# The state-space mixer's output projection in three rounded products, its low parts stored over the unturned rows

## The chip, the cores and the metric

One core of one Trainium2 chip runs the whole kernel. The metric is device microseconds per execution, lower is better. TensorE is called PE here, VectorE DVE, ScalarE ACT, GpSimd POOL and SyncE SP, as the profile does.

## The reference, cut to what matters

The reference is a network of two blocks on 256 tokens of width 1024, all float32. The second block has two layers; the mixer of its second layer is a bidirectional state-space model (SSD). The change concerns the last line of it, the output projection:

```python
def ssd_mixer(uc, ul, w_in, ..., norm_g, w_out, need_ctx):
    def run(h, s_init, need_y):
        z, xbc, dt = jnp.split(h @ w_in, [SSD_DI, SSD_DI + SSD_CONV_DIM], axis=-1)
        ...
        y = (y_f + y_b[:, ::-1] + xs * d_gr).reshape(b, l, SSD_DI)
        return rms_norm_2(y * jax.nn.silu(z), norm_g) @ w_out, (s_f, s_b)
```

y has 256 rows of 2048 columns, w_out is 2048 x 1024. The rows then go, in "snake" order, through a residual and a layer norm into a squared-ReLU MLP of width 4096.

## The kernel before, in words

The weights of the second block come in chunks of 2 MB. SP loads them into a ring of two slots, W, in the order of plan_chunks; each chunk in two halves of 1024 KB, as soon as the chunk two places ahead of it has been used (L2002 to L2018). For the chunks of the projection, named ("sy", n, c2) (n: half of the output columns, c2: half of the 2048 rows), "used" is the counter part_done for c2 = 0 and the bank ("sy", n, 1) being full for c2 = 1.

Ring (L101) plans the eight PSUM banks: claim waits until the bank's last use has been read, filled until it is full, read until it has been read. plan_block2 (L1581) gives every key its bank.

**The rounds.** The mixer has eight groups of four heads. All engines go through them in step, each in its own written order, and meet at semaphores:

- PE (L2470 to L2481), round g: group_outputs(g) (key "yo", 16 small products, then the two products of 512 columns, "yi", which need the last group's "yi" banks read), group_pre(g+1), group_gate(g+1) (the gate product "sz", 16 float32 products of 256 columns), group_turns(g-1), which turns the finished rows of a group by a product with the permutation, into the bank "yT".
- ACT (L2782 to L2788), round g: segments(g+1) (24 exponentials), state_copy(g+1), gate(g+1) (SiLU of "sz", with a table load), turned_out(g-1), which copies "yT" with the norm's gain into XTOK[:, 2:4].
- DVE (L3288 to L3295), round g: group_weights(g), diagonals(g+1), group_finish(g-1) (the rows of a group: skip, "yo", twice "yi" through YI, gate, squares), state_inputs(g+2).

**The projection.** out_part(n, c2) (L2455) multiplies, for both token tiles t and eight k each, a turned 128x128 tile of XTOK as the stationary operand with 512 columns of the raw chunk in W, all float32. The parts come as (0,0), the last group's turn, (0,1), a small product for the RMS ("rms"), (1,0), (1,1). DVE's residual("sy") (L2838, called at L3312) takes each full bank, scales it by the RMS factor, adds it to x and normalizes each token tile. In its last step sy_between (L3306) makes the first low pieces for the MLP and the low parts of its turned input.

**The MLP's way.** The MLP (ffn, L2163 and L2876) already works with rounded parts: ACT rounds a quarter chunk to float32r into WPH (high_parts, L2530), DVE subtracts it from the raw piece into WPL (low_part, L2871), and PE does three products for each one: high by high, high by low, low by high (L2174, L2191). ACT's order around it is L2789 to L2796: four high pieces, the two roots, split (the turned input with gain, and its rounded part UH), then the other pieces.

ARENA is one region of memory in which the tensors of each phase are carved over those of the last (L1831 to L1850): BDL and CDL first, XTOK (4 x 2048 columns: t = 0 and 1 the finished rows, 2 and 3 the other sequence's rows and later the turned ones), BTOK, SEGW, CBC and so on. The MLP's UH, WPH, UL and WPL lie over the same place.

Of the kernel before, what the change touches and what calls it, by code (L numbers as in the profile page):

```python
# [7 lines left out]
F32 = mybir.dt.float32  # L8
F32R = mybir.dt.float32r
I32 = mybir.dt.int32  # L10
ALU = mybir.AluOpType
# [1569 lines left out]
def plan_block2(full, empty):  # L1581
    r = Ring(full, empty)
    keys = []

    def turned(tag):
        return [("uT", tag, k) for k in range(KT)]

    def split(tag, nt):
        return [("uT", tag, s, j) for s in range(nt // 2) for j in range(4)]

    def plan_ffn(i):

        nt = 4 if i == 0 else 2
        sums = 0
        for kind, b, *rest in mlp_steps():
            if kind == "f1":
                r.plan(("f1", i, 4 * b + rest[0]), rest[0] % (2 if nt == 4 else 4))
            elif rest[1] == 1 and (nt == 4 or b == NB - 1):
                for t in range(nt):
                    r.plan(("f2", i, b, rest[0], t), 2 + sums % 6 if nt == 4 else 4 + sums)  # L1600
                    sums += 1

    keys += split("m0", 4)
    keys += [("ga",)] + [("gl", h, z) for h in range(GH) for z in range(2)]
    keys += [("gq", h) for h in range(GH)] + [("gk", h) for h in range(GH)]

    def along(what, n, ts):
        return [(what, n, t) for t in ts]

    def head_pre(h):  # L1610
        return [("kT", h, z) for z in range(2)] + [("A", h, z) for z in range(2)]

    def head_states(h):
        return [("kvs", h, n) for n in range(3)]

    def head_out(h):
        return [("go", h, s) for s in range(2)]

    for n, k in enumerate(keys):
        r.plan(k, n % 8)  # L1620
    beside = [head_pre(0), head_states(0) + head_pre(1), head_out(0) + head_states(1) + head_out(1),
              head_pre(2) + head_pre(3) + head_states(2) + head_states(3) + head_out(2) + head_out(3)]
    turn = 0
    for (what, half), heads in zip((("gv", 0), ("gv", 1), ("gg", 0), ("gg", 1)), beside):
        for n, k in enumerate(along(what, half, range(4))):
            r.plan(k, 1 + n)
        for k in heads:
            r.plan(k, (5, 6, 7, 0)[turn % 4])
            turn += 1
    keys = []  # L1630
    keys += turned("o0") + [("gy", n, t) for n in range(2) for t in range(4)]
    for n, k in enumerate(keys):
        r.plan(k, (1 + n) % 8)
    for k, b in zip(split("f0", 4), (1, 2, 3, 4, 0, 5, 6, 7)):
        r.plan(k, b)
    plan_ffn(0)
    r.plan(("cw",), 0)
    for (s, j), b in zip(((s, j) for s in range(2) for j in range(4)), (0, 1, 6, 7, 2, 3, 4, 5)):
        r.plan(("uT", "m1", s, j), b)
    keys = [("dt",), ("dtT",)]  # L1640
    conv = []
    for m in range(NX + 2 * SG_ + 1):
        if m == CUM_AT:
            conv += [("cum",), ("cd",)]
        if m < NX + 2 * SG_:
            conv.append(("sc", m))
        if 1 <= m <= NX + SG_:
            conv.append(("xt", m - 1))
    keys += conv
    for n, k in enumerate(keys):  # L1650
        r.plan(k, n % 8)

    def plan_group(g):
        r.plan(("cb", g), g % 2)
        r.plan(("ss", g), 2)
        r.plan(("sz", g), 3)

    plan_group(0)
    for g in range(SG_):
        r.plan(("yo", g), 4 + g % 2)  # L1660
        for t in range(2):
            r.plan(("yi", g, t), 6 + t)
        if g + 1 < SG_:
            plan_group(g + 1)
        if g >= 1:
            r.plan(("yT", g - 1), 2)
    r.plan(("yT", SG_ - 1), 2)
    r.plan(("rms",), 4)
    keys = [("sy", n, t) for n in range(2) for t in range(2)] + split("f1", 2)
    for n, k in enumerate(keys):  # L1670
        r.plan(k, n % 8)
    plan_ffn(1)
    return r
# [64 lines left out]
def block2(nc, io, c, XA, W, WLO, landed, dram_cum, dram_ada):  # L1738

    with ExitStack() as ctx:  # L1740
# [3 lines left out]
        def sem(name):  # L1744
            return ctx.enter_context(nc.semaphore(name))
# [37 lines left out]
        with ExitStack() as conv:  # L1783
            for name, n in (("ahead_of_XHI", 14336), ("XHI", 4096), ("ahead_of_PHI", 5120), ("PHI", 3072)):
                part = conv.enter_context(nc.sbuf_tensor(name, [P, n], F32R))
                if name == "XHI":
                    XHI = part[:].rearrange("p (k n) -> p k n", k=KT)
            PHI = part[:].rearrange("p (b k n) -> p b k n", b=3, k=KT)
        with ExitStack() as gla:
            for name, n in (("ahead_of_XHO", 16384), ("XHO", 4096)):  # L1790
                part = gla.enter_context(nc.sbuf_tensor(name, [P, n], F32R))
            XHO = part[:].rearrange("p (k n) -> p k n", k=KT)
# [118 lines left out]
        w_rdy = sem("b_segment_weights")  # L1911
        y_rdy = sem("b_ssd_out")
        rms_rdy = sem("b_ssd_squares")
        g_hi, g_lo = sem("b_gla_pieces_high"), sem("b_gla_pieces_low")
        g_part = sem("b_gla_partial_piece_used")
        g_xlow = sem("b_gla_x_low_part")
# [175 lines left out]
        def _(pe):  # L2092
# [359 lines left out]
                        last = mm(key, ((2 * q + t) * P, (2 * q + t + 1) * P), XTOK[:, t, k * P:(k + 1) * P], snake[:])  # L2452
                r.fill_done(last, key)

            def out_part(n, c2):  # L2455
                w = weights(("sy", n, c2))
                for t in range(2):
                    key = ("sy", n, t)
                    if c2 == 0:
                        r.claim(pe, key)  # L2460
                    for k in range(KT):
                        kk = c2 * KT + k
                        last = mm(key, (0, CHUNK), XTOK[:, 2 + kk % 2, (kk // 2) * SEQ + t * P:(kk // 2) * SEQ + (t + 1) * P], w[:, k, :],
                                  kk == 0, kk == 15)
                    if c2 == 1:
                        r.fill_done(last, key)
                if c2 == 0:
                    last.then_inc(part_done, 1)

# [5 lines left out]
            for g in range(SG_):  # L2475
# [3 lines left out]
                    group_gate(g + 1)  # L2479
                if g >= 1:  # L2480
                    group_turns(g - 1)  # L2481
            r.read(pe, ("yT", SG_ // 2 - 1))
            out_part(0, 0)
            group_turns(SG_ - 1)
            r.read(pe, ("yT", SG_ - 1))
            out_part(0, 1)
            pe.wait_ge(rms_rdy, 1)
            key = ("rms",)
            r.claim(pe, key)
            r.fill_done(mm(key, (0, 2), snake[:], ST[:, 2:4]), key)  # L2490
            out_part(1, 0)
            out_part(1, 1)
            ffn(1, 2, X_LN[1])

        @block.scalar
        def _(act):
# [270 lines left out]
            def turned_out(g):  # L2767
                key = ("yT", g)
                r.filled(act, key)
                b = bank[r.bank(key)]  # L2770
                for q in range(2):
                    k = 2 * g + q
                    last = nc.scalar.activation(XTOK[:, 2 + q, g * SEQ:(g + 1) * SEQ], b[:, q * SEQ:(q + 1) * SEQ], ACT.Copy,
                                                scale=NGC[:, k:k + 1])
                r.read_done(last, key)

            act.wait_ge(x_whole, 1)
            segments(0)
# [3 lines left out]
            for g in range(SG_):  # L2782
                if g + 1 < SG_:
                    segments(g + 1)
                    state_copy(g + 1)
                    gate(g + 1)
                if g >= 1:
                    turned_out(g - 1)  # L2788
            turned_out(SG_ - 1)  # L2789
            std(SQ_RMS, 0, 2)  # L2790
            high_parts(1, 0, PIECES)
            for t in range(2):
                std(SQ_LN[2] + t, t, t + 1)
            split("f1", 0, 1, 2, UH)
            high_parts(1, PIECES, len(STEPS_F))
            std(SQ_LN[3], 0, 2)  # L2796

        @block.vector
        def _(v):
# [453 lines left out]
            def group_finish(g):  # L3253
# [26 lines left out]
                for t in range(2):  # L3280
                    nc.vector.tensor_tensor_reduce(YI[:, t], xs[:, t], xs[:, t], 1.0 / SDI, 0.0, ALU.mult, ALU.add, RMS[:, t, g:g + 1])

            state_inputs(0)
            r.filled(v, ("sc", NX + 2 * SG_ - 1))
            nc.vector.tensor_tensor(UT[:, :, 0:SEQ], XLO[:, :, 0:SEQ].bitcast(F32), XHI[:, :, 0:SEQ].bitcast(F32), ALU.add).then_inc(x_whole, 1)
# [2 lines left out]
            for g in range(SG_):  # L3288
                group_weights(g)
                if g + 1 < SG_:  # L3290
                    diagonals(g + 1)
                if g >= 1:
                    group_finish(g - 1)
                if g + 2 < SG_:
                    state_inputs(g + 2)  # L3295
            group_finish(SG_ - 1)
            v.drain()
            nc.vector.tensor_reduce(ST[:, 2:4], RMS[:], AX, ALU.add).then_inc(rms_rdy, 1)
            r.filled(v, ("rms",))
            r.read_done(nc.vector.tensor_scalar(ST[:, 0:2], bank[r.bank(("rms",))][:, 0:2], RMS_EPS, None, ALU.add), ("rms",))  # L3300
            v.drain().then_inc(sq_in, 1)
# [2 lines left out]
            v.drain()  # L3304

            def sy_between(n, t):  # L3306
                if n == 1 and t == 1:
                    for q in range(2):
                        low_part(1, q)
                    lows(0, UH, UL, ul_done, 24)  # L3310
# [56 lines left out]
```

## Time and profile before

| | |
|---|---|
| Median of three runs | 2330.67 us (2325.55 to 2337.14) |
| Profiled execution | 2340.91 us, its span 2339.3 us |
| Mean granted clock of PE | 0.948 of full speed |
| PE busy | 2077.0 us (89%), 12086 matmul records |
| DVE busy | 1204.2 us (51%) |
| ACT busy | 727.7 us (31%) |
| POOL busy | 167.0 us (7%) |

The durations below come from the profiled execution, whose time is 10.24 us above the median of the runs. Times of day are microseconds from the start of the span. The state-space rounds lie from about 1947 to 2074, the projection from there to 2131, the last MLP from there to the end. Records of matmuls overlap: the engine is pipelined, and the start-to-start distance is what one costs. One float32 matmul shows as two records.

### The profile page before, as it was taken

Reading aid. Unit: us, or ns where it says so; the run is one execution under the profiler, and the core shown is the slowest. Engines: PE = TensorE matmul, PEld = TensorE weight load, DVE = VectorE, ACT = ScalarE, POOL = GpSimd, SP = SyncE. Lnnn points to the kernel's source line nnn. Section 1 sums busy time; section 2 is a strip of 40 time slices with the busy share of each in tenths; the row PEclk is TensorE's granted clock in tenths of the full one; section 3 lists DMA queues with packets and bytes.
Section 4 is the critical chain, followed back from the end, with each engine's and each line's share of the span. In section 5 each row is a group of like instructions: output and inputs, shape, how many; then the busy total and the mean of one; then the engine's idle time right before and its main releaser. Section 6 shows DMA issues by size and latency. Waiting matters only on the chain.

```text
span 2339.3 us, 32520 instructions
## 1 busy us (share of the span) xinstructions
PE 2077.0 (89%) x12086; PEld 1470.9 (63%) x12086; DVE 1204.2 (51%) x2131; ACT 727.7 (31%) x1317; POOL 167.0 (7%) x155
## 2 busy tenths in 40 slices
PE   6999888888998748886999899999989988998997
PEld 4787432325786412333788778888877776765996
DVE  3464411115463401114738587666666886745766
ACT  3453200103452200003433331221135545722332
POOL 2001100001001100002441300000000000000000
PEclk9989999999999969998999899999999998999999
DMA  7459699984469669984221223222222234324552
GB/s 226 154 209 330 236 404 389 391 312 134 170 235 338 247 262 359 400 320 154 71 77 67 77 90 126 108 85 96 80 99 73 92 128 142 126 73 160 191 191 107
DMA packets 151940, 440.42 MB, mean 188 GB/s; under 512 B 10368, under 2 KB 12848, under 8 KB 143456
## 3 DMA queue, kind: packets, MB, share of 16 engines
q1 hardware_dynamic: 143424, 415.87, 47.9%
q0 software_dynamic: 8352, 22.39, 3.3%
q8 instruction: 101, 1.65, 0.3%
q14 instruction: 63, 0.52, 0.1%
HBM read 534.52 MB, written 1.21 MB: 229 GB/s over the span
## 4 chain that ended last, share of the span: by engine, by line
PE 40%; DVE 6%; ACT 4%; DVEq 2%; issue 1%; DMA 1%; ACTq 0%; POOL 0%; SPq 0%; POOLq 0%
PE bank L2101 24%; PE bank L2192 11%; PE bank L2243 4%; DVE ARENA L3211 1%; ACT ARENA L2753 1%; PE bank L2106 1%; DVEq L2827 0%; ACT UT L2524 0%; ACTq L2527 0%; DVE XA L2828 0%; DMA W<-in_ffn_w 0%; ACT ARENA L2746 0%; DVEq L3213 0%; ACT ARENA L2501 0%; DVE XA L2826 0%
## 5 line engine op out<-in xcount | busy, mean ns | idle before, releaser
L2537 ACT ACTIVATE WPH<-W 128x1024 fp32r<-128x1024 f32 x128 | 135.5, 1063 | 399.5 <-PE bank L2101 199.9
L2101 PE MATMUL bank<-UH,WPH 128*128 128x512 f32 (+1 forms) x512 | 174.5, 341 | 5.6 <-DVE WPL L2873 2.4
L2101 PE MATMUL bank<-UL,WPH 128*128 128x512 f32 (+1 forms) x512 | 173.2, 338 | 0.0
L2101 PE MATMUL bank<-UH,WPL 128*128 128x512 f32 (+1 forms) x512 | 173.0, 338 | 0.0
L2873 DVE TENSOR_TENSOR WPL<-W,WPH 128x1024 fp32r<-128x1024 f32 x128 | 153.6, 1219 | 17.8 <-ACT WPH L2537 17.8
L1426 DVE TENSOR_TENSOR H<-SG,bank 128x256 f32<-128x256 f32 x24 | 10.1, 421 | 289.7 <-ACT SG L1013 289.7
L2192 PE MATMUL bank<-WPH,MHH 128*128 128x512 f32 x384 | 149.5, 389 | 0.0
L2192 PE MATMUL bank<-WPL,MHH 128*128 128x512 f32 x384 | 149.5, 389 | 0.0
L2192 PE MATMUL bank<-WPH,MHL 128*128 128x512 f32 x384 | 149.4, 389 | 0.0
L675 PE MATMUL bank<-W,XG 128*32 128x512 f32 x768 | 98.6, 660 | 50.3 <-DMA W<-in_expert_w_up 38.8
L2101 PE MATMUL bank<-ARENA 128*128 128x64 f32 (+4 forms) x528 | 108.9, 367 | 19.2 <-DVEq L3251 7.6
L675 PE MATMUL bank<-WA,XG 128*32 128x512 f32 x768 | 95.6, 642 | 24.7 <-DMA WA<-in_expert_w_up 24.7
L2101 PEld LDWEIGHTS bank<-UH,WPH 128*128 128x128 f32 x512 | 98.2, 192 | 19.4 <-issue 3.7
L2101 PEld LDWEIGHTS bank<-ARENA 128*128 128x128 f32 (+1 forms) x528 | 83.4, 211 | 39.6 <-issue 19.5
L712 PE MATMUL bank<-WC,H 128*32 128x512 f32 x768 | 89.0, 604 | 21.1 <-DMA WC<-in_expert_w_down 15.4
L1013 ACT ACTIVATE SG<-bank 128x256 f32<-128x256 f32 x24 | 9.2, 383 | 314.9 <-PE bank L675 314.9
L2101 PEld LDWEIGHTS bank<-UL,WPH 128*128 128x128 f32 x512 | 98.3, 192 | 10.1
L2101 PEld LDWEIGHTS bank<-UH,WPL 128*128 128x128 f32 x512 | 98.3, 192 | 10.0
L2101 PE MATMUL bank<-XHI,PHI 128*128 128x512 f32 (+2 forms) x264 | 99.9, 378 | 3.5 <-DVE XLO L2835 2.4
L508 PE MATMUL bank<-W,XT 128*128 128x512 f32 x192 | 89.9, 629 | 11.5 <-DMA W<-in_w_in 7.1
L2101 PE MATMUL bank<-XHI,WLO 128*128 128x512 f32 (+2 forms) x264 | 97.5, 369 | 0.0
L675 PEld LDWEIGHTS bank<-W,XG 128*32 128x32 f32 x768 | 25.2, 119 | 114.5 <-issue 66.7
(445 smaller groups left out, 4341.1 us busy)
## 6 DMA issues: line engine op xcount, KB each, us to landing
WC<-in_expert_w_down SPq DMA_DIRECT2D x32, 2048.0 KB
W<-in_ffn_w SPq DMA_DIRECT2D x64, 1024.0 KB, 6.6
W<-in_ada_w SPq DMA_DIRECT2D x48, 1024.0 KB, 7.3
WA<-in_expert_w_gate SPq DMA_DIRECT2D x16, 2048.0 KB
WA<-in_expert_w_up SPq DMA_DIRECT2D x16, 2048.0 KB
W<-in_expert_w_gate SPq DMA_DIRECT2D x16, 2048.0 KB
W<-in_expert_w_up SPq DMA_DIRECT2D x16, 2048.0 KB
WC<-in_expert_w_down SPq DMA_DIRECT2D x32, 1024.0 KB
```

Source lines behind the costliest of these rows:

```text
L508: last = nc.tensor.matmul(bank[r.bank(key)][:, 0:n], lhs[k], rhs[k], start=(k == 0), stop=(k == len(lhs) - 1))
L675: last = nc.tensor.matmul(bank[r.bank(key)][32 * g:32 * g + 32, :], xg[:, 4 * part + k, col:col + 32], WA[part][:, g, :, k, :], start=(par ...
L712: last = nc.tensor.matmul(bank[r.bank(key)][32 * g:32 * g + 32, :], H[i // MQ][:, f, 32 * g:32 * g + 32], WC[:, g, f, n * CHUNK:(n + 1) * ...
L1426: r.read_done(nc.vector.tensor_tensor(H[q // MQ][:], SG[q // MQ][:].rearrange("p (n f) -> p f n", f=2), bank[r.bank(key)][:, EH:2 * EH].re ...
L2101: return nc.tensor.matmul(bank[r.bank(key)][0:rows, cols[0]:cols[1]], lhs, rhs, start=start, stop=stop)
L2106: return nc.tensor.transpose(bank[r.bank(key)][0:m, j * P:j * P + k], src, ident[0:k, 0:k])
L2192: last = nc.tensor.matmul(bank[r.bank(key)][:, :], a, x[:, k, :], start=first and k == 0 and z == 0, stop=last_block and kp == 1 and k == ...
L2243: last = nc.tensor.matmul(bank[r.bank(key)][:, :], x[:, kk, tok], a[:, k, :], start=kp == 0 and k == 0 and z == 0, stop=kp == 3 and k == 1 ...
L2537: nc.scalar.activation(piece_view(WPH, q), piece_src(i, q), ACT.Copy).then_inc(hi_done, 1)
L2753: last = nc.scalar.activation(SEGD[:, jt, z, h, :], SEGD[:, jt, z, h, :], ACT.Exp, bias=NCUM[:, jt, col:col + 1])
L2873: nc.vector.tensor_tensor(piece_view(WPL, q), piece_src(i, q), piece_view(WPH, q).bitcast(F32), ALU.subtract).then_inc(lo_done, 1)
L3211: last = nc.vector.scalar_tensor_tensor(acc, src, CW[:, m, k:k + 1], acc, ALU.mult, ALU.add)
```

## The change

Both operands of the projection are taken apart into a rounded (float32r) high part and the low rest, and each product becomes three. The parts and their places:

- YH is the turned rows' high part, in the place of XTOK[:, 2:4], written by ACT in turned_out. YL is the low part, in the place of XTOK[:, 0:2], the finished but unturned rows, of which a group is free once it is turned. DVE writes it in a new turned_low(g), out of the same bank, after turned_out(g).
- SYH0, SYH1 and SYH2 take the high part of a chunk of weights, written by ACT in four pieces (out_weights_high); the low part goes to the slot of WLO, by DVE (out_weights_low).
- The bank "yT" is now read by DVE after ACT, and moves from bank 2 to g % 2 (3 for group 6).
- In the rounds, turned_low(g-2) stands on DVE between diagonals(g+1) and group_finish(g-1).
- out_part takes pairs of k and waits for each pair's low parts; (1,1) is done first for token tile 0, then for tile 1.
- On ACT two high pieces of the MLP instead of four come ahead of the split, and they wait for the end of the projection.

```diff
@@ plan_block2
-            r.plan(("yT", g - 1), 2)
+            r.plan(("yT", g - 1), g % 2 if g < SG_ - 1 else 3)
@@ block2
+        with ExitStack() as mixed:
+            SYH2 = mixed.enter_context(nc.sbuf_tensor("SYH2", [P, KT, CHUNK], F32R))
+            YL, YH = [mixed.enter_context(nc.sbuf_tensor(name, [P, 2, SG_ * SEQ], F32R)) for name in ("YL", "YH")]
+            SYH = [mixed.enter_context(nc.sbuf_tensor(f"SYH{q}", [P, KT, CHUNK], F32R)) for q in range(2)] + [SYH2]
@@ PE
-            def out_part(n, c2):
-                w = weights(("sy", n, c2))
-                for t in range(2):
-                    key = ("sy", n, t)
-                    if c2 == 0:
-                        r.claim(pe, key)
-                    for k in range(KT):
-                        kk = c2 * KT + k
-                        last = mm(key, (0, CHUNK), XTOK[:, 2 + kk % 2, (kk // 2) * SEQ + t * P:(kk // 2) * SEQ + (t + 1) * P], w[:, k, :],
-                                  kk == 0, kk == 15)
-                    if c2 == 1:
-                        r.fill_done(last, key)
+            def out_part(n, c2, ts=range(2), kps=range(4)):
+                ci = SY.index((n, c2))
+                lo = WLO[:, number[("sy", n, c2)] % SLOTS]
+                for kp in kps:
+                    pe.wait_ge(sy_lo, 4 * ci + kp + 1)
+                    pe.wait_ge(yl_rdy, 4 * c2 + kp + 1)
+                    for t in ts:
+                        key = ("sy", n, t)
+                        if c2 == 0 and kp == 0:
+                            r.claim(pe, key)
+                        for k in (2 * kp, 2 * kp + 1):
+                            kk = c2 * KT + k
+                            c0 = (kk // 2) * SEQ + t * P
+                            for z, (y, w) in enumerate(((YH, SYH[ci % 3]), (YH, lo), (YL, SYH[ci % 3]))):
+                                last = nc.tensor.matmul(bank[r.bank(key)][:, :], y[:, kk % 2, c0:c0 + P], w[:, k, :],
+                                                        start=kk == 0 and z == 0, stop=kk == 15 and z == 2, skip_group_check=True)
+                        if c2 == 1 and kp == 3:
+                            r.fill_done(last, key)
                 if c2 == 0:
                     last.then_inc(part_done, 1)
...
-            r.read(pe, ("yT", SG_ // 2 - 1))
             out_part(0, 0)
             group_turns(SG_ - 1)
-            r.read(pe, ("yT", SG_ - 1))
             out_part(0, 1)
...
             out_part(1, 0)
-            out_part(1, 1)
+            out_part(1, 1, (0,))
+            out_part(1, 1, (1,))
@@ ACT
-                    last = nc.scalar.activation(XTOK[:, 2 + q, g * SEQ:(g + 1) * SEQ], b[:, q * SEQ:(q + 1) * SEQ], ACT.Copy,
+                    last = nc.scalar.activation(YH[:, q, g * SEQ:(g + 1) * SEQ], b[:, q * SEQ:(q + 1) * SEQ], ACT.Copy,
                                                 scale=NGC[:, k:k + 1])
-                r.read_done(last, key)
+                last.then_inc(yh_rdy, 1)
+
+            def out_weights_high(ci):
+                n = number[("sy", *SY[ci])]
+                act.wait_ge(landed[n % SLOTS], 32 * (n // SLOTS + 1))
+                if ci == 1:
+                    r.filled(act, ("yo", SG_ - 1))
+                if ci == 2:
+                    r.filled(act, ("yi", SG_ - 1, 1))
+                if ci == 3:
+                    act.wait_ge(part_done, 1)
+                for kp in range(4):
+                    if ci == 0 and kp == 2:
+                        r.filled(act, ("yo", SG_ - 2))
+                    nc.scalar.activation(SYH[ci % 3][:, 2 * kp:2 * kp + 2, :], W[:, n % SLOTS, 2 * kp:2 * kp + 2, :], ACT.Copy).then_inc(sy_hi, 1)
...
+                if g == SG_ - 1:
+                    out_weights_high(0)
                 if g >= 1:
                     turned_out(g - 1)
+            out_weights_high(1)
             turned_out(SG_ - 1)
+            out_weights_high(2)
             std(SQ_RMS, 0, 2)
-            high_parts(1, 0, PIECES)
-            for t in range(2):
-                std(SQ_LN[2] + t, t, t + 1)
+            out_weights_high(3)
+            std(SQ_LN[2], 0, 1)
+            r.filled(act, ("sy", 1, 1))
+            high_parts(1, 0, 2)
+            std(SQ_LN[2] + 1, 1, 2)
             split("f1", 0, 1, 2, UH)
-            high_parts(1, PIECES, len(STEPS_F))
+            high_parts(1, 2, len(STEPS_F))
@@ DVE
+            def turned_low(g):
+                key = ("yT", g)
+                v.wait_ge(yh_rdy, g + 1)
+                for q in range(2):
+                    k = 2 * g + q
+                    last = nc.vector.scalar_tensor_tensor(YL[:, q, g * SEQ:(g + 1) * SEQ], bank[r.bank(key)][:, q * SEQ:(q + 1) * SEQ],
+                                                          NGC[:, k:k + 1], YH[:, q, g * SEQ:(g + 1) * SEQ].bitcast(F32), ALU.mult, ALU.subtract)
+                r.read_done(last, key)
+                v.drain().then_inc(yl_rdy, 1)
+
+            def out_weights_low(ci):
+                n = number[("sy", *SY[ci])]
+                for kp in range(4):
+                    v.wait_ge(sy_hi, 4 * ci + kp + 1)
+                    nc.vector.tensor_tensor(WLO[:, n % SLOTS, 2 * kp:2 * kp + 2, :], W[:, n % SLOTS, 2 * kp:2 * kp + 2, :],
+                                            SYH[ci % 3][:, 2 * kp:2 * kp + 2, :].bitcast(F32), ALU.subtract).then_inc(sy_lo, 1)
...
                 if g + 1 < SG_:
                     diagonals(g + 1)
+                if g >= 2:
+                    turned_low(g - 2)
                 if g >= 1:
                     group_finish(g - 1)
...
+            out_weights_low(0)
             group_finish(SG_ - 1)
+            turned_low(SG_ - 2)
             v.drain()
             nc.vector.tensor_reduce(ST[:, 2:4], RMS[:], AX, ALU.add).then_inc(rms_rdy, 1)
+            out_weights_low(1)
+            turned_low(SG_ - 1)
+            out_weights_low(2)
...
             def sy_between(n, t):
+                if n == 0 and t == 1:
+                    out_weights_low(3)
```

## Rows read from the trace of the kernel before

**Rows 1.** The page: the span, and busy time and share by engine.

```profile
span 2339.3 us, 32520 instructions
PE 2077.0 (89%) x12086; PEld 1470.9 (63%) x12086; DVE 1204.2 (51%) x2131; ACT 727.7 (31%) x1317; POOL 167.0 (7%) x155
```

**Rows 2.** Busy time by stretch: three rounds, the projection, two stretches around stalls.

```profile
core 0: us, PE busy (x) PEld busy (x) DVE busy (x) ACT busy (x) POOL busy (x), PEclk, DMA share, GB/s
1985.67:2001.51 15.84, 15.84 (x85) 12.90 (x84) 12.21 (x26) 11.49 (x30) 1.05 (x2) 1.00 0.18 57
2001.51:2018.36 16.85, 15.86 (x85) 12.90 (x84) 14.22 (x29) 11.49 (x30) 1.05 (x2) 1.00 0.58 196
...
2051.05:2066.89 15.84, 15.84 (x85) 12.90 (x84) 10.86 (x22) 11.49 (x30) 0.00 (x0) 1.00 0.00 1
...
2089.00:2131.00 42.00, 41.31 (x98) 18.38 (x98) 7.97 (x15) 6.11 (x9) 0.00 (x0) 1.00 0.42 150
...
1760.00:1770.00 10.00, 6.83 (x33) 5.31 (x32) 6.14 (x11) 6.80 (x9) 0.00 (x0) 1.00 0.00 0
2162.20:2165.60 3.40, 3.32 (x16) 3.32 (x17) 2.99 (x7) 0.00 (x0) 0.00 (x0) 0.51 0.46 164
```

**Rows 3.** PE in order of time: start, us; in brackets the idle time before.

```profile
2007.08 2.82 PE L2101 MATMUL bank<-ARENA 128*128 128x512 f32 x8 [0.99 <-DVE YI L3268]
...
2073.97 13.90 PE L2101 MATMUL bank<-W,ARENA 128*128 128x512 f32 x32
...
1764.13 0.66 PE L2106 MATMUL bank<-ident,ARENA 128*128 128x128 f32 x4 [3.17 <-ACT ARENA L2716]
...
2162.28 0.58 PE L2101 MATMUL bank<-UH,WPH 128*128 128x256 f32 x1 [2.39 <-DVE WPL L2873]
```

**Rows 4.** The chain that ended last: start, us, what.

```profile
2039.77 49.00 PE bank L2101 x220
...
2089.68 41.70 PE bank L2101 x98
...
2162.28 7.42 PE bank L2101 x48
2169.71 10.91 PE bank L2192 x48
2180.61 11.51 PE bank L2101 x96
```

**Rows 5.** Groups of instructions by form, PE, from 2073.9 to 2131.5.

```profile
L2101 PE MATMUL bank<-W,ARENA 128*128 128x512 f32 x128 | 55.6, 594 | 0.9 <-ACT ARENA L2773 0.9
```

**Rows 6.** ACT in order of time.

```profile
2018.61 1.28 ACT L2501 ACT_TABLE_LOAD   x1 [5.32 <-PE bank L2101]
...
2020.39 0.83 ACT L2773 ACTIVATE ARENA<-bank,NGC 128x256 f32<-128x256 f32 x2
...
2125.68 3.90 ACT L2537 ACTIVATE WPH<-W 128x1024 fp32r<-128x1024 f32 x4 [21.40 <-DMA W<-in_ffn_w]
```

**Rows 7.** DVE in order of time.

```profile
2003.47 0.76 DVE L3260 TENSOR_TENSOR ARENA<-ARENA,DROW 128x256 f32<-128x256 f32 x2
...
2004.92 0.75 DVE L3268 TENSOR_TENSOR YI<-bank,EC 128x256 f32<-128x256 f32 x2
...
2066.23 0.76 DVE L3260 TENSOR_TENSOR ARENA<-ARENA,DROW 128x256 f32<-128x256 f32 x2
...
2072.42 0.76 DVE L3260 TENSOR_TENSOR ARENA<-ARENA,DROW 128x256 f32<-128x256 f32 x2
...
2131.41 0.75 DVE L2850 SCALAR_TENSOR_TENSOR ARENA<-bank,ST,MB 128x512 f32<-128x512 f32 x1 [0.66 <-PE bank L2101]
...
2144.00 1.22 DVE L2873 TENSOR_TENSOR WPL<-W,WPH 128x1024 fp32r<-128x1024 f32 x1
...
2173.08 4.62 DVE L2873 TENSOR_TENSOR WPL<-W,WPH 128x1024 fp32r<-128x1024 f32 x4
```

**Rows 8.** SP's DMA issues in order of time.

```profile
2117.67 14.65 SPq L2018 DMA_DIRECT2D W<-in_ffn_w  x4
```

More of the change, by code:

```diff
@@ L1913, in block2 @@
         rms_rdy = sem("b_ssd_squares")
+        yh_rdy, yl_rdy = sem("b_ssd_turned_high"), sem("b_ssd_turned_low")
+        sy_hi, sy_lo = sem("b_ssd_out_weights_high"), sem("b_ssd_out_weights_low")
+        SY = [(n, c2) for n in range(2) for c2 in range(2)]
         g_hi, g_lo = sem("b_gla_pieces_high"), sem("b_gla_pieces_low")
```

## The prediction, made before the change was run

> **What bounds the kernel now.** The page comes first: TensorE (PE) is busy for 89% of the span, so a saving on PE may count, but only where PE is the last to finish [rows 1]. The stage table then splits the eight rounds over the state-space groups. From the end of one gate product to the end of the next a round lasts 15.84 or 16.85 us, 15.84 to 15.86 of it PE, at a granted clock of 1.00 [rows 2]. So PE bounds the rounds, but barely: the 1.0 us missing in every other round is a wait on VectorE (DVE) in the PE timeline, just before the products called "yi" [rows 3]. The DVE step named there is a product written to YI out of a bank (L3268), and in the chain of waits PE alone goes on from that point through the output projection, except for the 0.9 us from 2088.77 to 2089.68, in which ScalarE (ACT) copies the last turned group [rows 4]. After the projection the chain goes by DVE and ACT into the MLP.
>
> **The projection itself: a gain.** The four parts of out_part are 64 float32 matmuls of 512 columns, which the trace shows as 128 records, 55.6 us in all, 13.85 a part from start to start [rows 5]. The change makes 192 rounded ones of them, in the pattern that L2192 has already (high by high, high by low, low by high): 48 of those take 10.91 us at full clock [rows 4]. So each part falls from 13.85 to 10.91 us; over four parts this saves 11.8 us. The loads of weights are hidden in both rows' pace. The trace thus says 0.79 of the old time. The Trainium skill ("FP8 and Floating Point Precision", TensorE Precision Notes) counts true FP32 as four passes; three of four would give 0.75, a saving of 13.9 us instead of 11.8, and the sum below would be 2.1 us better. The trace has a row for each form, so 0.79 stands.
>
> **Splitting the weights.** ACT rounds each chunk in 4 pieces, 3.90 us by the same copies ahead of the MLP [rows 6]; DVE subtracts in 4 pieces, 4.62 us [rows 7]. That is 15.6 us of ACT and 18.5 of DVE more. Between 2089 and 2131 they are busy for only 7.97 (DVE) and 6.11 us (ACT) [rows 2], and PE needs a quarter of a chunk only every 2.73 us (10.91 / 4), where DVE makes one in 1.15 (4.62 / 4). That hides behind PE except at the first piece of a part, below. Each chunk still follows its slot's release: SP issues at 2117.67, and ACT, waiting for the landing, starts at 2125.68, 8.0 us later [rows 6, 8].
>
> **The low rows, in the round: a loss.** Each round g from 2 to 7 now has turned_low(g-2) on DVE ahead of group_finish(g-1). It waits for turned_out(g-2), which ACT does only after gate(g). Behind that wait stands the finish, and for the finish's reads of YI waits PE's "yi" of round g. I follow one round, counted from the end of gate(g) on PE (the turn at 2018.36):
> - ACT: table load from 2018.61, gate copy, turned copies to 2021.22, so 2.86 us after that end [rows 2, 6].
> - DVE: turned_low, two scalar_tensor_tensors of 256 columns out of a bank. No row has that form from a bank; the pair at L3268 takes 0.75 us, and twice the one of 512 columns at L2850 would be 1.50 [rows 7]. I take 0.85, nearest to the pair, and 0.13 for drain and hand-over: the finish starts at 3.84.
> - From the finish's start to PE's "yi": 2003.47 to 2007.08, 3.61 us [rows 3, 7].
> - PE from "yi" to the end of the next gate: 2007.08 to 2018.36, 11.28 us [rows 2, 3].
>
> Together 18.73 us, a circle PE, ACT, DVE, PE in which nothing overlaps. Before, DVE began the finish at 2003.47, 1.96 us after the gate's end [rows 2, 7], without asking ACT. No slack covers this: PE already waits, or just doesn't, at "yi". So each of the six rounds has a PE stall of 18.73 - 15.85 = 2.9 us. What else ACT and DVE do in a round (they are busy for 11.49 and at most 14.22 us of it [rows 2]) then ends before PE asks for it, and leaves the chain.
>
> Place by place: gate(2) ends at 1985.67 as before. Five rounds of 18.73 put the end of gate(7) at 2079.32 (before 2066.89 [rows 2]), and with the sixth stall "yi" of group 7 starts at 2086.8. turned_low(5) and finish(6) then end at 2089.35, since a finish takes 6.19 us (2066.23 to 2072.42) [rows 7]; DVE's first low piece (1.2) lets PE begin the projection at 2090.55, against 2073.97 before [rows 3]. **This costs 16.6 us.**
>
> **From there on.** Part (0,0) ends at 2101.5 and the last turn at 2102.4. DVE has meanwhile done low(0), finish(7), turned_low(6), the sum, and the first piece of low(1) at 2102.6; part (0,1) goes from there to 2113.6. The old 0.9 us wait for ACT is gone: the last group's low rows (2107) are needed only at 2110.8. Chunk (1,0) lands at 2101.5 + 8 = 2109.6, its first low piece is there at 2111.9, PE asks at 2113.7. Chunk (1,1) lands at 2121.6; its first low piece waits rather for the two residuals of n = 0 (three steps like L2850's 0.75 us each [rows 7]) and comes at 2123.9, PE asks at 2124.6. Both fit, by 1.8 and 0.7 us. Part (1,1) by token halves ends at 2135.5, against 2131.4 [rows 4, 7]: **4.1 us later.** This is 16.6 lost, 11.8 gained by the matmuls, some 0.7 by the smaller waits. The bank changes cost nothing: every new claim comes after a read that precedes YI's on DVE.
>
> **Into the MLP.** Only two high pieces are rounded before the split now; the third follows it on ACT and takes 1.0 us (3.90 / 4), so DVE's low piece starts 0.4 us later than in the old order, where it began at 2144.00 right behind the last low part of x [rows 7], and this is on the chain. +0.4. Sum: **+4.5 us** at an undisturbed clock. Its bounds: turned_low from 0.75 to 1.5 us, six times, is -0.6 to +3.9, so +3.9 to +8.4.
>
> **The clock.** Six stalls of 2.9 us are new. A stall of 2.39 us was followed by a stretch at 0.51, the lower level, 1.2 GHz, and 48 matmuls took 7.42 us there against 5.76 (half of 11.51), a loss of 1.7; a stall of 3.17 us after denser work left the clock at 1.00 [rows 2 to 4]. I let two of the six stalls end so: +3.4. The Trainium skill ("TensorE: Matmul & The Clock Gate", HAM oscillation) says that only longer idle gaps than these throttle it; by that rule nothing is added and the time would be 2335.2. The trace has a counterexample at 2.39 us, so the measurement decides.
>
> Forecast: 4.5 + 3.4 = +7.9 us. The rows are of one execution with 2340.91 us (span 2339.3 [rows 1]); the median of the runs is 2330.67, and the difference is set upon that: **2338.5 us**.
>
> **Rivals.**
> 1. The clock stays up in all six stalls: +4.5, 2335.2 us. For it: the 3.17 us stall [rows 3]. Chance 0.17.
> 2. Slower beyond doubt: the stalls throttle in nearly every round. Six times 1.7 on the circle is +10.0, with 4.5 together +14.5, 2345.2 us; from the fifth on it exceeds 0.5%. For it: the shorter stall of 2.39 us did it [rows 3]; against it, each is followed by 15.8 us of dense work. The dear turned_low belongs here too. Chance 0.27.
> 3. Faster: the wait on ACT doesn't reach PE, because finish(g-1) finds its reads done early enough. Then the sum is -11.8 - 0.7 + 0.4 = -12.1, 2318.6 us. For it: PE's share, 89%. Against it: PE waited there even before [rows 3]. Chance 0.07.
> 4. Forecast as above, one to four throttled stalls: 0.49.
>
> That the change doesn't do what it says, I see no way for: the number of matmuls follows from the loops.
>
> **How the numbers follow.** A measurement of this kernel tells about 0.5%, 11.7 us, from nothing. Faster by more: rival 3, 0.07, less a little because it lies so near the bound: 0.06. Slower by more: rival 2's 0.27 and the upper edge of the forecast, 0.05: 0.32. The rest, 0.62, is the same. Range: from 2324 (below rival 1, since three runs spread over 2325 to 2337) to 2350 (rival 2 with a dear turned_low in part); rival 3 and the far end of rival 2 are left out.
>
> **What would show it.** Rounds 3 to 7, end of gate to end of gate: 18.7 us each (right) or 16 (rival 3). PE idle ahead of "yi" about 2.9 us, DVE idle ahead of turned_low, for ACT, 3 to 4 us once the rounds have settled. The four parts: 192 matmuls, 43.6 us. PE's first sy matmul at about 2090.6, its last at 2135.5. Clock below 1.00 in some rounds. I am wrong if the rounds keep 16 us, or if PE waits for low pieces or landings inside parts (1,0) and (1,1).

## The result, and the profile after

| | before | changed |
|---|---|---|
| Median of ten runs each | 2330.02 us | 2342.97 us |
| Ratio, 95% interval | | 1.0063 [1.0046, 1.008] |
| Span of the profiled execution | 2339.3 us | 2346.0 us |
| PE busy | 2077.0 us | 2065.6 us |
| DVE busy | 1204.2 us | 1229.0 us |
| ACT busy | 727.7 us | 743.6 us |

The change makes the kernel slower by 0.63%, 14.7 us of 2330, although PE is busy for 11.4 us less. (The ratio isn't the quotient of the two medians, which are 12.95 us or 0.56% apart; that lies within its interval.) The rounds show why. First the busy time by stretch, from the end of one gate product to the end of the next, from gate(2) to gate(7) (they answer to [rows 2]), then the stretch up to shortly before the first matmul of the projection:

```profile
core 0: us, PE busy (x) PEld busy (x) DVE busy (x) ACT busy (x) POOL busy (x), PEclk, DMA share, GB/s
1976.63:1997.97 21.34, 18.39 (x85) 14.13 (x84) 14.83 (x30) 11.61 (x30) 1.05 (x2) 0.84 0.14 50
1997.97:2018.46 20.49, 17.54 (x85) 13.78 (x84) 14.00 (x28) 11.61 (x30) 1.05 (x2) 0.92 0.45 154
2018.46:2038.96 20.50, 17.55 (x85) 13.76 (x84) 14.00 (x28) 11.61 (x30) 1.05 (x2) 0.92 0.16 52
2038.96:2059.46 20.50, 17.55 (x86) 13.75 (x85) 14.00 (x28) 11.61 (x30) 0.00 (x0) 0.92 0.30 103
2059.46:2079.95 20.49, 17.54 (x85) 13.73 (x84) 10.25 (x20) 11.61 (x30) 0.00 (x0) 0.92 0.00 0
2079.95:2091.20 11.25, 8.30 (x50) 6.54 (x49) 7.65 (x17) 6.39 (x8) 0.00 (x0) 0.87 0.53 188
```

A round takes 20.5 us (the first 21.3) where it took 15.8 or 16.9. Two things are new in it. PE is idle for 2.95 us (20.50 less 17.55), and its busy time has itself grown from 15.86 to 17.55 us, because the mean clock of the round is 0.92 instead of 1.00. Both stand in the PE timeline of one round:

```profile
2018.46 1.05 PE L2108 MATMUL bank<-snake_perm,ARENA 128*128 128x128 f32 x8
2019.36 3.68 PE L2108 MATMUL bank<-ARENA 128*128 128x64 f32 x32
2025.99 4.51 PE L2108 MATMUL bank<-ARENA 128*128 128x512 f32 x8 [2.95 <-DVE YI L3301]
2030.34 1.88 PE L2108 MATMUL bank<-MB,ARENA 128*128 128x512 f32 x4
2032.06 7.07 PE L2108 MATMUL bank<-W,UT 128*128 128x256 f32 x32
```

The eight records of "yi" and "cb" behind the stall take 4.51 us; they took 2.82 [rows 3]. The 1.7 us more are the lower clock, right after the idle time. Behind the first stall, the stretch shows it without a mixture: 0.50, the lower level, 1.2 GHz.

```profile
1984.15:1987.50 3.35, 3.35 (x4) 1.48 (x5) 3.03 (x10) 3.35 (x12) 0.00 (x0) 0.50 0.00 0
```

The other stalls of the six are as long (2.95 us) and were all followed by the lower level: 5.36 us for these eight records behind the first, 4.51 behind the next four, and 2.98 for the last group's four (1.98 at full clock in the run filler3, below). The chain of waits shows the circle, one turn of it:

```profile
2018.71 0.87 ACT L2514
2019.58 0.42 issue
2020.00 0.60 ACT ARENA L2514
2020.60 0.74 ACT YH L2786 x2
2021.36 0.48 DVE YL L3321
...
2022.38 0.43 DVE ARENA L3293
...
2025.99 13.15 PE bank L2108 x44
```

PE ends the gate, ACT loads its table, copies the gate and then the turned rows (YH); only then DVE makes the low rows (YL) and starts the finish. From "yi" on PE has 13.15 us of work to the end of the next gate. DVE has been waiting for ACT all the while, as its timeline shows:

```profile
2013.28 2.50 DVE L3269 TENSOR_TENSOR ARENA<-ARENA,NEGM 128x512 f32<-128x512 f32 x4
2021.36 0.88 DVE L3321 SCALAR_TENSOR_TENSOR YL<-bank,NGC,YH 128x256 fp32r<-128x256 f32 x2 [5.59 <-ACT YH L2786]
2022.38 0.76 DVE L3293 TENSOR_TENSOR ARENA<-ARENA,DROW 128x256 f32<-128x256 f32 x2
```

The projection did get its gain. The groups by form, from 2088 to 2139 (against [rows 5]), and the chain from the first part on:

```profile
L2477 PE MATMUL bank<-SYH,YH 128*128 128x512 f32 x64 | 25.5, 398 | 0.2 <-DVE WLO L3330 0.2
L2477 PE MATMUL bank<-WLO,YH 128*128 128x512 f32 x64 | 25.4, 396 | 0.0
L2477 PE MATMUL bank<-SYH,YL 128*128 128x512 f32 x64 | 25.2, 394 | 0.0
```

```profile
2091.99 11.09 PE bank L2477 x48
2103.08 0.89 PE bank L2108 x8
2103.97 11.12 PE bank L2477 x48
2115.11 0.37 SPq L2025
2115.52 8.63 DMA W<-in_ssd_w_out
2124.18 1.07 ACT SYH L2802
2125.27 1.24 DVE WLO L3330
2126.55 11.48 PE bank L2477 x48
2138.05 0.75 DVE ARENA L2883
```

A part takes 11.1 us instead of 13.9. The busy times of the three groups overlap and can't be added. For one part, the last, the chain goes by its chunk's landing; the wait it leaves on PE is short, 0.16 us idle in the timeline.

Where the time went, from the places above and those of before [rows 2 to 4, 7]:
- From the end of gate(2) to that of gate(7): 81.22 us (1985.67 to 2066.89) became 103.32 (1976.63 to 2079.95), +22.1.
- From there to the first projection matmul: 7.08 (to 2073.97) became 11.80 (to 2091.75), +4.7.
- The projection until DVE takes the last bank: 57.44 (to 2131.41) became 46.30 (to 2138.05), -11.1.
- From there to the end of the span: 207.9 both times.

That is +15.7 us. The rest of the difference of the spans, -9.0, lies ahead of gate(2), in code that the change doesn't touch. How much that code varies from one execution to the next can be read off the nine kept traces: gate(2) ends anywhere between 1966.97 and 1985.67. The stretch from there to the last bank's read (145.74 us before, 161.42 changed) leaves that out, and is used below beside the ratios, as what one execution of each kernel shows.

### The profile page after: what moved, and what is told of

It reads as the page before. It is cut to its first block, busy times and chain, and to the rows that moved or that the text cites. A ratio compares the mean times of both kernels' runs of the same rounds, so it can differ in the third digit from the quotient of the medians.

```text
span 2346.0 us, 32725 instructions
## 1 busy us (share of the span) xinstructions
PE 2065.6 (88%) x12150; PEld 1486.1 (63%) x12150; DVE 1229.0 (52%) x2163; ACT 743.6 (32%) x1333; POOL 166.9 (7%) x155
## 4 chain that ended last, share of the span: by engine, by line
PE 40%; DVE 6%; ACT 3%; DVEq 2%; issue 1%; DMA 1%; ACTq 0%; SPq 0%; POOL 0%; POOLq 0%
PE bank L2108 23%; PE bank L2199 11%; PE bank L2250 4%; PE bank L2477 1%; DVE ARENA L3244 1%; PE bank L2113 1%; ACT ARENA L2514 0%; DVEq L2860 0%; DMA W<-in_ssd_w_out 0%; ACT UT L2537 0%; ACTq L2540 0%; DVE XA L2861 0%; DMA W<-in_ffn_w 0%; DVEq L3246 0%; DVE XA L2859 0%
## 5 line engine op out<-in xcount | busy, mean ns | idle before, releaser
L2108 PE MATMUL bank<-ARENA 128*128 128x64 f32 (+4 forms) x528 | 119.5, 390 | 34.7 <-DVE YI L3301 17.7
L675 PE MATMUL bank<-WA,XG 128*32 128x512 f32 x768 | 88.9, 604 | 24.8 <-DMA WA<-in_expert_w_up 24.8
L2108 PE MATMUL bank<-XLO,PHI 128*128 128x512 f32 (+2 forms) x264 | 97.2, 368 | 0.0
```

The source lines that it names most:

```text
L675: last = nc.tensor.matmul(bank[r.bank(key)][32 * g:32 * g + 32, :], xg[:, 4 * part + k, col:col + 32], WA[part][:, g, :, k, :], start=(par ...
L2108: return nc.tensor.matmul(bank[r.bank(key)][0:rows, cols[0]:cols[1]], lhs, rhs, start=start, stop=stop)
```

## The experiments

The seven variants were timed against the kernel before on the same chip. The medians of before there were 2328.25 us (low_rows_inside to before_wait) and 2327.62 us (low_rows_behind to before_time); the row of the changed kernel is that of the result, with 2330.02 us before. So the ratios are what to compare between rows, and not the medians. The last column is the stretch in each profiled execution from the end of gate(2) to DVE's start on the last bank of the projection. The theories: **A**, the wait for ACT's copy closes a circle through PE, ACT and DVE, and its stalls also lower the clock. **B**, what costs is DVE's 1.0 us for the low rows, wherever it stands. **C**, the whole added work is too much for ACT and DVE.

| kernel | ratio to before, 95% | median us | gate(2) to last bank, us |
|---|---|---|---|
| before | | | 145.74 |
| changed | 1.0063 [1.0046, 1.008] | 2342.97 | 161.42 |
| low_rows_inside | 0.9954 [0.9936, 0.9971] | 2316.37 | 134.70 |
| no_low_rows | 0.9963 [0.9945, 0.998] | 2315.64 | 134.73 |
| filler3 | 1.0028 [1.0013, 1.0043] | 2331.99 | 150.97 |
| before_wait | 1.0084 [1.0066, 1.0103] | 2344.47 | 163.20 |
| low_rows_behind | 0.9958 [0.9936, 0.998] | 2320.16 | 140.34 |
| filler1 | 1.0043 [1.0022, 1.0064] | 2337.42 | 158.00 |
| before_time | 1.0028 [1.0008, 1.0048] | 2334.42 | 154.90 |

### low_rows_inside: the same work, behind the read that PE waits for

```diff
-                if g >= 2:
-                    turned_low(g - 2)
                 if g >= 1:
-                    group_finish(g - 1)
+                    group_finish(g - 1, g - 2 if g >= 2 else None)
@@ group_finish(g, low=None)
                         if z == 1:
                             r.read_done(last, key)
+                    if z == 1 and low is not None:
+                        turned_low(low)
                     v.drain()
                     nc.vector.tensor_tensor(xs, xs, YI[:], ALU.add)
```

> turned_low(g-2) moves on DVE from ahead of group_finish(g-1) to within it, behind the second read of the yi banks; all else as in the changed kernel. Theory A (the circle PE, ACT, DVE, PE that the wait for the turned copy closes costs 2.95 us a round, and each stall lowers the clock for another 1.7): rounds go back to 15.8 and 16.9 us at a granted clock of 1.00, the first sy matmul comes about 123 us after the first yo matmul instead of 149, and the whole takes about 26 us less than the changed kernel, about 2318, ratio to before 0.995. Theory B (the price is the DVE time of the low rows, 1.0 us a round, wherever it stands): the rounds stay longer than 16.9 us, ratio near 1.005. Theory C (DVE and ACT get too much work in all): PE waits for weight pieces or exponents in the rounds, ratio about 1.00.

Measured: ratio 0.9954 [0.9936, 0.9971], where the changed kernel has 1.0063: 25 us faster than that, 11 us faster than the kernel before. Of the versions that make the whole output it has the lowest ratio. Three of its rounds:

```profile
1976.41:1992.27 15.86, 15.86 (x85) 12.90 (x84) 13.03 (x28) 11.48 (x30) 1.05 (x2) 1.00 0.18 60
1992.27:2009.11 16.84, 15.86 (x86) 12.90 (x85) 14.98 (x31) 11.49 (x30) 1.05 (x2) 1.00 0.59 194
2009.11:2024.96 15.85, 15.85 (x85) 12.90 (x84) 13.01 (x28) 11.49 (x30) 1.05 (x2) 1.00 0.18 56
```

These are the rounds of before to 0.02 us, with the low rows made in them (DVE is busy for 13.0 and 15.0 us instead of 12.2 and 14.2). B falls: the same DVE work costs nothing in the rounds once the read that PE waits for comes first. C falls as well.

### no_low_rows: the ceiling

```diff
-                if g >= 2:
-                    turned_low(g - 2)
...
-            turned_low(SG_ - 2)
...
-            turned_low(SG_ - 1)
...
-                last.then_inc(yh_rdy, 1)
+                r.read_done(last, key)
...
-                    pe.wait_ge(yl_rdy, 4 * c2 + kp + 1)
+                    r.read(pe, ("yT", 4 * c2 + kp))
...
-                            for z, (y, w) in enumerate(((YH, SYH[ci % 3]), (YH, lo), (YL, SYH[ci % 3]))):
+                            for z, (y, w) in enumerate(((YH, SYH[ci % 3]), (YH, lo), (YH, SYH[ci % 3]))):
```

> The changed kernel without turned_low: the low rows are not made, the third product reads the high rows instead, so the low rows' share is left out of the output; the number of matmuls and the weights' parts are as in the changed kernel. Theory A: rounds of 15.8 and 16.9 us, clock 1.00, the four parts 46 us, about 2318 us, ratio 0.995. Theory B: the same here, so this run gives the ceiling that the other one is held against; if the ratio is above 1.00, the loss is in the projection or the weights, not in the rounds.

This kernel leaves the low rows out: its third product reads the high rows again, and its output lacks their share. Measured: 0.9963 [0.9945, 0.998]. This and low_rows_inside can't be told apart by their ratios, and the stretch from gate(2) to the last bank is 134.73 us here and 134.70 there. So low_rows_inside has all there is to get by making the low rows free, and the loss of the changed kernel against it (161.42 us in that stretch) lies in where the low rows stand.

### filler3 and filler1: work instead of idleness

```diff
                 r.read(pe, ("ss", g))
+                for _ in range(3 if g >= 2 else 0):
+                    nc.tensor.matmul(bank[2][:, :], CDL[:, g, 0:P], SSB, start=True, stop=True)
```

filler1 has 1 in place of 3.

> The changed kernel with three more float32 matmuls of 512 columns a round, on rounds 2 to 7, between the yo products and the yi products, into the bank of the states, which is free there: 2.6 us of PE work inside a stall of 2.95 us. Theory A with the clock lowered by idleness: stall 0.35 us or so, clock 1.00 in rounds 3 to 7, a round 18.8 us instead of 20.5, some 10 us less than the changed kernel, ratio to before about 1.002. Rival: the lower clock has another cause than the idle PE; then the rounds stay at 20.5 us or grow, ratio 1.006 or more.

> As filler3 with one filler matmul a round instead of three: 0.87 us of work in the stall, 2.1 us of it left idle. before_wait had stalls of 1.94 us, of which about half were followed by the lower clock. If the idle length decides: rounds of 18.8 us and of 20.5 us mixed, 2 to 4 of the six lowered, 3 to 7 us less than the changed kernel, ratio about 1.004. If any work in the stall is enough: as filler3, ratio 1.0028. If none: as the changed kernel, 1.006.

filler3 measured 1.0028 [1.0013, 1.0043], 8 us below the changed kernel by the ratios and 10.5 by the stretch from gate(2) to the last bank, with 18 float32 matmuls more. Two of its rounds and its stall:

```profile
1985.71:2004.44 18.73, 18.50 (x91) 13.88 (x90) 13.99 (x28) 11.61 (x30) 1.05 (x2) 1.00 0.49 168
2004.44:2023.18 18.74, 18.51 (x91) 13.88 (x90) 14.00 (x28) 11.61 (x30) 1.05 (x2) 1.00 0.17 57
```

```profile
2011.88 2.85 PE L2108 MATMUL bank<-ARENA 128*128 128x512 f32 x8 [0.23 <-DVE YI L3303]
```

The round is 18.74 us, the circle without its clock price, and the clock is at 1.00 in all five rounds. So the lower clock came of PE's idleness, and cost 1.76 us a round (2.60 in the first). filler1 measured 1.0043 [1.0022, 1.0064]. In its profiled execution 1.94 us were left idle:

```profile
1982.32:2001.06 18.74, 16.80 (x88) 13.12 (x86) 14.82 (x30) 11.61 (x30) 1.05 (x2) 1.00 0.17 57
2001.06:2021.49 20.43, 18.48 (x87) 13.74 (x86) 13.99 (x28) 11.61 (x30) 1.05 (x2) 0.92 0.45 154
```

Of the five rounds shown by the stretches, the first was at 1.00 and the four others at 0.92. The sixth group's four records took 3.57 us against 1.98 in filler3, so that five of six stalls were followed by the lower clock, where I had expected two to four. This execution was the slowest of the twelve (2334 to 2350 us), and the spread of some 15 us leaves room for others with fewer; the ratio lies where it was expected, but its interval overlaps those of filler3 and of the changed kernel, so only the trace tells them apart.

### before_wait and before_time: the wait and the work, each alone, in the kernel before

```diff
+                if g >= 2:
+                    r.read(v, ("yT", g - 2))
                 if g >= 1:
                     group_finish(g - 1)
```

> The kernel before, with nothing added but a wait: in rounds 2 to 7 DVE waits, ahead of group_finish(g-1), until ACT has copied the turned rows of group g-2. No low rows, no rounded products. Theory A: rounds of 17.8 us at full clock (2.95 + 3.61 + 11.28), a PE stall of 2.0 us ahead of yi, projection 10 us later than before, and up to 20 us later if each stall lowers the clock; ratio 1.004 to 1.009. Theory B (it is the DVE time of the low rows, not the wait): rounds as before, ratio 1.000.

```diff
+                if g >= 2:
+                    for q in range(2):
+                        xs = XTOK[:, q, (g - 1) * 256:g * 256]
+                        nc.vector.scalar_tensor_tensor(YI[:, q], xs, NGC[:, q:q + 1], xs, ALU.mult, ALU.subtract)
+                    v.drain()
                 if g >= 1:
                     group_finish(g - 1)
```

> The kernel before, with two idle scalar_tensor_tensors of 256 columns and a drain (1.0 us of DVE) in the place of turned_low, in rounds 2 to 7, and no wait: DVE time alone. Theory A: the chain ACT, DVE, PE of two rounds grows by 1.0 us, PE stalls of 1 to 2 us in every other round, 3 us in all, ratio 1.001, against 1.0084 for the wait alone. Theory B, that DVE's time is what costs: ratio 1.004 or more.

before_wait, one wait and no work, costs as much as the whole change does on balance, with the gain in the projection counted: 1.0084 [1.0066, 1.0103] against 1.0063 [1.0046, 1.008]. Four of the five stretches from gate(2) to gate(7), the fourth left out:

```profile
1971.32:1992.07 20.75, 18.81 (x86) 14.29 (x85) 14.06 (x28) 11.61 (x30) 1.05 (x2) 0.84 0.13 52
1992.07:2012.68 20.61, 18.67 (x85) 14.29 (x84) 13.22 (x26) 11.61 (x30) 1.05 (x2) 0.83 0.44 153
2012.68:2030.48 17.80, 15.86 (x86) 12.91 (x85) 13.22 (x26) 11.50 (x30) 1.05 (x2) 1.00 0.17 60
...
2048.27:2067.76 19.49, 17.55 (x86) 13.65 (x85) 9.38 (x18) 11.61 (x30) 0.00 (x0) 0.91 0.00 0
```

17.80 us at full clock is the circle without the low rows, as worked out. The low rows' own DVE time adds the rest, 0.94 us a round, to the 18.74 of filler3. The stalls of these five rounds are 1.94 us long; three of the rounds were slowed, by 1.69 to 2.95 us of PE time (the fourth was like the third, at 1.00, and the sixth stall, 1.92 us, was followed by 1.00 too).

before_time's two idle operations take 0.88 us, as turned_low's do, though they don't read a bank. It measured 1.0028 [1.0008, 1.0048], where I had written 1.001. Its stretches:

```profile
1967.11:1985.62 18.51, 17.55 (x85) 13.49 (x84) 15.64 (x32) 11.62 (x30) 1.05 (x2) 0.91 0.18 58
1985.62:2001.29 15.67, 15.67 (x85) 12.83 (x84) 11.37 (x24) 11.49 (x30) 1.05 (x2) 1.00 0.55 190
2001.29:2022.14 20.85, 18.73 (x85) 14.28 (x84) 18.99 (x39) 11.61 (x30) 1.05 (x2) 0.84 0.17 60
```

```profile
1972.65 4.51 PE L2101 MATMUL bank<-ARENA 128*128 128x512 f32 x8 [0.96 <-DVE YI L3268]
2007.99 5.46 PE L2101 MATMUL bank<-ARENA 128*128 128x512 f32 x8 [2.12 <-DVE YI L3268]
```

The stalls are in every other round and as long as expected (0.96, then 2.12 us). What I had left out is again the clock: each was followed by the lower level. The ratio's interval holds both the 1.001 of theory A and the 1.004 of theory B, so it doesn't decide between them. It lies clear of before_wait's, so the wait costs more than DVE's time at this place. The time isn't free there either: the stretch from gate(2) to the last bank is 9.2 us longer than before, against 17.5 us for the wait.

### low_rows_behind: the low rows behind the whole finish

```diff
-                if g >= 2:
-                    turned_low(g - 2)
                 if g >= 1:
                     group_finish(g - 1)
+                if g >= 2:
+                    turned_low(g - 2)
```

> turned_low(g-2) on DVE right behind group_finish(g-1), so later than in low_rows_inside. The wait for ACT is gone here too, but the bank of the turned rows is also that of the next group's cb product, which PE claims 1.7 us after yi. Theory A with the bank as a second bound: turned_low ends 7.2 us after the finish begins, PE asks at 5.3, a stall of about 1.9 us in most rounds, now ahead of cb; two rounds together take 34.5 us instead of 32.7; some 5 us more than low_rows_inside, up to 12 where the clock falls, 2321 to 2329, ratio 0.997 to 1.001. Rival: only the wait on ACT matters, DVE's place behind it is free; then as low_rows_inside, 0.995.

Measured: 0.9958 [0.9936, 0.998], median 2320.16 us against low_rows_inside's 2316.37. I had expected 0.997 to 1.001; the ratio came out below that, nearer to the rival's 0.995, and the intervals don't separate the two versions. The trace does: the stretch from gate(2) to the last bank is 5.6 us longer than in low_rows_inside. The stall has moved ahead of "cb" and names the low rows:

```profile
1976.54 1.13 PE L2108 MATMUL bank<-ARENA 128*128 128x256 f32 x4 [1.56 <-DVE YL L3321]
...
1993.38 1.13 PE L2108 MATMUL bank<-ARENA 128*128 128x256 f32 x4 [0.91 <-DVE YL L3321]
```

Its rounds last 17.68 and 16.84 us by turns, 34.52 a pair as worked out, 86.73 the five (81.25 in low_rows_inside), and the clock stayed at 1.00 in all of them. Two of them:

```profile
1968.45:1986.13 17.68, 16.12 (x86) 12.82 (x84) 14.92 (x30) 11.49 (x30) 1.05 (x2) 1.00 0.16 61
1986.13:2002.97 16.84, 15.93 (x85) 12.74 (x84) 13.25 (x28) 11.49 (x30) 1.05 (x2) 1.00 0.54 187
```

## Why the prediction was right in its range and short in its size

The range (2324 to 2350) holds the measured 2342.97. The forecast was 2338.5, +7.9 us where 14.7 came, and the outcome it called likeliest, within 0.5% (0.62), was missed by a little: rival 2, with 0.27, is what happened. The mechanism was right; the term for the clock was too small. Point by point:

- **The circle.** Right, place by place. From the end of the gate to the start of the finish 3.92 us (predicted 3.84; turned_low took 0.88, not 0.85), from there to "yi" 3.61 (3.61), the stall 2.95 (2.9). At full clock, in filler3, the round is 18.74 us (18.73).
- **The clock.** Here the forecast failed. The term "I let two of the six stalls end so: +3.4" should have been six: 12.97 us from "yi" to the end of the gate (2025.99 to 2038.96) where 11.28 was put, in four rounds, and 13.82 in the first. With six times 1.7 the same sum gives 4.5 + 10.2 = 14.7 us, which is what the ratio says. That this fits so well is partly luck. Against filler3 the first stall's clock cost 2.60 us, the next four 1.76 each, and the sixth only 0.41, since at full clock PE waits 0.89 us for DVE's first low piece instead (11.39 us from gate(7) to the projection there, 11.80 in the changed kernel): 10.0 us in all. And the trace shows +15.7 us up to the last bank, not 14.7. I had weighed one stall of 2.39 us that lowered the clock against one of 3.17 us that didn't, and leaned on the "15.8 us of dense work" between one new stall and the next. But just ahead of the stall stands the "yo" group, 32 records of 64 columns; that it matters is only argued.
- **Rival 1**, that the clock stays up, had 0.17 and is out: six of six stalls of 2.95 us were followed by the lower level, and so was one of 0.96 us in before_time. By the rule of the Trainium skill ("TensorE: Matmul & The Clock Gate", HAM oscillation), that only longer idle gaps than these throttle the clock, rival 1 would have come true; the traces disagree.
- **The projection.** -11.1 us measured from the first matmul to the last bank's reader, against -11.8 and -0.7 predicted for it. A part is 11.1 us, not 10.91, and the last one waited a little: 0.16 us of PE idle for its first low piece, a small case of what the prediction gave as a sign of being wrong. Chunk (1,1) landed 9.1 us after its slot came free (2115.11 to 2124.18), not 8.0, and the landing, not the residuals (done at 2122.4), set that piece.
- **Start of the projection.** The extra 16.6 us were counted without the clock, and filler3, at full clock, has 16.8 (93.69 + 11.39 us against 81.22 + 7.08). With the clock 22.1 + 4.7 = 26.8 was measured.
- **Into the MLP.** Predicted +0.4, and not found. DVE does wait 0.25 us for the third high piece (below), but the low parts of x now begin 6.67 us after the last bank's read instead of 7.13, and this low piece starts 12.48 us after it instead of 12.59. The stretch from the projection to the end is unchanged to 0.1 us.
- **Rival 3**, that the wait doesn't reach PE, is out by the 2.95 us in every round. What it was to give, 2318.6 us, is close to what low_rows_inside gives (2316.37) by taking the wait out of the way.

```profile
2150.53 1.23 DVE L2906 TENSOR_TENSOR WPL<-W,WPH 128x1024 fp32r<-128x1024 f32 x1 [0.25 <-ACT WPH L2550]
```

## What to carry to other kernels

Before placing an operation in a strict queue, look for what stands behind it and whose wait that ends: here 1.0 us of DVE work a round added nothing to five rounds (81.25 us against 81.22) behind the last read of the banks that PE needs, 5.5 us behind the finish, and 22 us ahead of it, where it also brought in a wait on ACT and, after each stall, the lower clock. A stall on PE should be priced with the clock that follows it. A gain of 11 us in one stage says nothing for the kernel until the stage that feeds it has been followed round by round.

## What was not expected of the hardware

Short idle times lower PE's clock more readily than the one trace of before suggested. Ahead of "yi", behind the 64-column products: 2.95 us, six of six; 1.94 us, three of six in before_wait and five of six in filler1; 0.96 us, once in before_time, while the kernel before had such stalls of 0.99 us at a clock of 1.00 [rows 2, 3], and low_rows_inside of 0.98 us. So the length of the stall alone doesn't decide. Ahead of "cb", behind 512-column products, 1.56 and 0.91 us in low_rows_behind left it at 1.00 in all five rounds. The price each time is 1.7 us of PE work or more (4.51 to 5.46 us for eight records that take 2.82). Whether the kind of work ahead of a stall or the moment at which it comes decides was not tried by itself and stays open.
